# One copy of the split down weights and a third raw slot for down weights in a mixture-of-experts kernel

## The chip, the cores and the metric

The kernel runs on one core of a Trainium2 chip. The metric is the device time of one execution in microseconds; three runs of the kernel before are given, and the median counts. A core has TensorE (PE in the profile; its weight loads are PEld), VectorE (DVE), ScalarE (ACT) and GpSimd (POOL), each with a queue of its own that is worked in order. The sync engine (SP) computes nothing; it waits on semaphores and issues DMAs.

## What is computed

One layer of a streaming encoder over 1088 tokens of width 1024: an input LayerNorm, a token mixer (a state-space group and a short-convolution group), a projection with LayerNorm and router, a mixture of 64 experts with 6 per token, a shared expert, and a last LayerNorm. The change is about the routed experts:

```python
def expert_block(args):
    tok, e = args                       # the rows of 128 slots, one expert
    xb = h_pad[tok]
    hid = jax.nn.silu(xb @ w_gate[e]) * (xb @ w_up[e])
    return hid @ w_down[e]

yb = lax.map(expert_block, (row_tok.reshape(n_blocks, MOE_BLOCK), block_e))
yb = yb.reshape(rows, d) * row_w[:, None].astype(yb.dtype)
return jax.ops.segment_sum(yb, row_tok, num_segments=t + 1)[:t]
```

`w_gate[e]` and `w_up[e]` are 1024x256, `w_down[e]` is 256x1024, all float32: 1 MB each, 3 MB an expert. An expert gets one block of 128 slots or more, as its tokens need.

## The kernel before

The program is a row of stages with a barrier between them: trunk, mixing, output (gating and projection), experts, final LayerNorm. `expert_stage` (L1851) holds the loop.

A float32 product is made of three products in a reduced float format: a matrix is split into a high part (ScalarE copies it to the reduced type) and a low part (VectorE subtracts the high part from the original), and TensorE sums high x high, high x low and low x high. So every weight passes this way: DMA into a raw slot, high copy by ScalarE, low copy by VectorE, then matmuls from the two copies. A raw slot is free once the low part of its last block has been made.

- Raw slots: `raw_up` has `UP_SLOTS` = 3 slots (gate and up weights of one expert, 2 MB), `raw_dn` has `DN_SLOTS` = 2 (1 MB each). They are placed before `project_stage`, because that stage already fetches for the experts: `prefetch` (L1278) loads gate and up of experts 0 to 2 and down of experts 0 and 1.
- Split copies: `up_h`, `up_l` for two blocks (`par` is the block's parity), and `dn_h`, `dn_l` for two blocks as well.
- Experts are put in an order by `order_experts`; what is called expert e below is the one at place e. A table in `keep.small` tells each engine what block n needs: `THIRD` (its up slot, e mod 3), `ODD` (its down slot, e mod 2), the arrival counts `IN0` and `IN1`, `ENDS` (how many blocks there are up to the end of an expert) and `ORDER` (which expert stands at a place). `block_counts` (L1757) works the columns out on VectorE in a chain of small instructions, and TensorE turns them into rows (`turn_tables`).

Here the routing gives 77 blocks for 64 experts. `over_blocks` (L1898) runs `body(n)` for each block on every engine, each in its own order:

- TensorE: gate/up product of block n (`up`, 24 matmuls), transpose of the hidden values of n-1, transpose of the gathered tokens of n+2 (`turn_x`), down product of n-2 (`down`, 12 matmuls).
- ScalarE: SiLU of n (L1981), high hidden part of n-1, high token part of n+2 (L1992), high gate weights of n+2 (L1963, waits for the DMA of both gate and up weights), high down weights of n-1 (`down_high`, L2009), output copy of n-2 (L1986), high up weights of n+2 (L1963).
- VectorE: hidden values of n, low hidden part of n-1, low token part of n+2, low gate weights of n+2 (L2146), low down weights of n-1 (`down_low`, L2167), low up weights of n+2 (L2146).
- GpSimd: gather of the token rows of block n+4 (L2045), scatter with addition of the results of n-2 (L2054). Both are DMAs of GpSimd's own queue.
- SP: one expert at a time, and in order. For place e it first issues `down(e - 3)`, then `gate_up(e)`:

```python
def down(e, odd, until):
    expert = entry(sp, ORDER, e, N_EXP - 1)
    wait(sp, dn_l_done, until)
```

`until` is `ends(e - AHEAD)` with `AHEAD = UP_SLOTS + DN_SLOTS` = 5 for the down load at place e (L1937), and `ends(e - UP_SLOTS)` on `up_l_done` for the gate/up load (L1927). Each load also waits until the load two experts before it has arrived, since the two arrival semaphores are shared by parity.

`down_high(n)` waits with `wait(act, down_done, n - 1)`: the down product of block n-2, the last reader of its copy of `dn_h` and `dn_l`, must be over. In `project_stage` the scale and shift rows of the LayerNorm, `lng` and `lnb`, are two tensors of 128x1024; once the LayerNorms are done, parts of `lng` serve as scratch for the tables.

Of the kernel before, what the change touches and what calls it, by code (L numbers as in the profile page):

```python
# [6 lines left out]
ALU = mybir.AluOpType  # L7
# [6 lines left out]
P = 128  # L14
D = 1024
# [25 lines left out]
DN_SLOTS = 2  # L41
# [30 lines left out]
def chain(eng, own):  # L72


    count = {}

    def link(ins, sem=own):
        count[sem] = count.get(sem, 0) + 1
        ins.then_inc(sem, 1)
        eng.wait_ge(sem, count[sem])  # L80
    return link

# [1110 lines left out]
def project_stage(nc, io, keep, w, rt):  # L1193


    with ExitStack() as ctx:
        m = Pools(nc, ctx, "proj")
        gT, ycT = keep.gT, keep.ycT
        lng, lnb = m.sb("lng", [P, D]), m.sb("lnb", [P, D])
# [34 lines left out]
        whole, third, odd, both, in0, in1 = (m.sb(n, [P, 1]) for n in ("whole", "third", "odd", "both", "in0", "in1"))  # L1234
        even_i, evens, trip = m.sb("even_i", [1, 64], I32), m.sb("evens", [1, 64]), m.sb("trip", [1, 1])
# [30 lines left out]
        def _(sp):  # L1266
# [11 lines left out]
            def prefetch(e):  # L1278
# [5 lines left out]
                if e < DN_SLOTS:  # L1284
                    sp.dma_start(rt.raw_dn[:, e, :, :], io.w_down[0, e].rearrange("(p k) n -> p k n", p=P)).then_inc(
                        rt.down_in[e % 2], 16)
# [162 lines left out]
        def _(pe):  # L1449
# [98 lines left out]
            def turn_tables():  # L1548
                pe.wait_ge(s_eo, 1)
                for k, col in enumerate((in0, in1, third, odd)):  # L1550
# [44 lines left out]
        def _(v):  # L1595
# [161 lines left out]
            def block_counts():  # L1757

                for slot, n in ((third, UP_SLOTS), (odd, 2)):
# [3 lines left out]
                    link(stt(out=slot[:, :], in0=whole[:, :], scalar=-float(n), in1=eo[:, :], op0=ALU.mult, op1=ALU.add))  # L1763
                link(ts(both[:, :], eo[:, :], 8.0, 16.0, ALU.mult, ALU.add))
# [86 lines left out]
def expert_stage(nc, io, keep, rt):  # L1851

    with ExitStack() as ctx:
# [8 lines left out]
        dn_h, dn_l = m.sb("dn_h", [P, 2, 2, D], F32R), m.sb("dn_l", [P, 2, 2, D], F32R)  # L1862
# [20 lines left out]
        IN0, IN1, THIRD, ODD, ENDS, ORDER = range(6)  # L1883
# [39 lines left out]
        def _(sp):  # L1923
# [10 lines left out]
            def down(e, odd, until):  # L1934
# [5 lines left out]
                sp.dma_start(raw_dn[:, odd, :, :], w_d[bass.ds(expert, 1)].rearrange("a p k n -> (a p) k n")).then_inc(down_in[odd], 16)  # L1940
# [5 lines left out]
            LOOP = UP_SLOTS * DN_SLOTS  # L1946
            peeled = N_EXP - (N_EXP - AHEAD) // LOOP * LOOP
            for e in range(UP_SLOTS, peeled):
                if e >= AHEAD:
                    down(e - UP_SLOTS, (e - UP_SLOTS) % 2, ends(e - AHEAD))  # L1950
                gate_up(e, e % UP_SLOTS, e % 2, ends(e - UP_SLOTS))
            with sp.Fori(peeled, N_EXP - LOOP + 1, LOOP) as b:
                for u in range(LOOP):
                    e = peeled + u
                    down(b + (u - UP_SLOTS), (e - UP_SLOTS) % 2, ends(b + (u - AHEAD)))
                    gate_up(b + u, e % UP_SLOTS, e % 2, ends(b + (u - UP_SLOTS)))
            for e in range(N_EXP - UP_SLOTS, N_EXP):
                down(e, e % 2, ends(e - DN_SLOTS))

        @block.scalar  # L1960
        def _(act):
# [39 lines left out]
            def down_high(n, par):  # L2001
                in0, in1 = arrivals(act, n)
                slot = entry(act, ODD, n, DN_SLOTS - 1)
                wait(act, down_done, n - 1)
# [366 lines left out]
```

## Time and profile before

| | |
|---|---|
| device time, three runs | 1499.12, 1499.76, 1502.8 us; median 1499.76 |
| the profiled execution: span from first to last instruction | 1505.0 us; no other time of it is recorded |
| busy in the span: PE, DVE, ACT, POOL | 1278.8 us (85%), 1124.8 (75%), 875.4 (58%), 777.0 (52%) |
| expert loop, first to last SiLU | 662.87 to 1428.78 us |
| moved by DMA in the whole span | 334.94 MB |
| DMA issue to landing, median: gate, up, down weights | 9.3, 13.1, 8.1 us |
| the same for gathers, scatters | 11.4, 12.4 us |

Starts are us from the start of the span. A row of the timeline gives start, duration, engine, line and operation, and in brackets how long the engine was idle before it and what ended that. The busy share of the DMA is the mean over the core's 16 DMA engines of the time that packets were in flight there; with many transfers at once it reads a little over 1. TensorE's granted clock (PEclk) is a share of full speed.

### The profile page before, as it was taken

How to read it: one execution, taken by the hardware profiler on the slowest of the kernel's cores; microseconds unless marked ns; L12 is line 12 of the kernel's file. 1: busy time of each engine (PE TensorE's matmuls, PEld its weight loads, DVE VectorE, ACT ScalarE, POOL GpSimd, SP SyncE). 2: the span in 40 equal slices, each digit the busy share in tenths (PEclk: the TensorE clock that was granted, in tenths of full speed). 3: DMA queues.
4: the chain of work that ended last, by engine and by line, in shares of the span. 5: the costliest groups of instructions: out<-in, count | busy, mean ns of one | idle time of the engine just before them, and what ended most of it. 6: DMA issues, size and time to landing. Idle time of an engine off the chain costs nothing. (4 is left out here: it accounts for less than half of the span.)

```text
span 1505.0 us, 24140 instructions
## 1 busy us (share of the span) xinstructions
PE 1278.8 (85%) x6387; PEld 1086.6 (72%) x6387; DVE 1124.8 (75%) x1442; ACT 875.4 (58%) x1043; POOL 777.0 (52%) x643
## 2 busy tenths in 40 slices
PE   4787889986699989669999999999999999999920
PEld 3787888983488868558887778787877778787810
DVE  6925758743678976459988888887988888888828
ACT  7521201205535542148887778887877778887735
POOL 1017765804600136225765667676766667665720
PEclk9898989997799999879999999999999999999975
DMA  9233315256422354147899999999999989999647
GB/s 279 103 95 52 83 21 100 60 40 238 159 99 112 109 197 144 60 159 241 325 350 331 340 312 346 332 318 335 326 346 321 340 308 344 335 317 344 161 141 280
DMA packets 114164, 334.94 MB, mean 223 GB/s; under 512 B 30736, under 2 KB 61456, under 8 KB 89536
## 3 DMA queue, kind: packets, MB, share of 16 engines
q1 hardware_dynamic: 88928, 280.51, 52.5%
q0 software_dynamic: 24752, 53.73, 14.3%
q8 instruction: 26, 0.43, 0.1%
q14 instruction: 26, 0.21, 0.0%
q10 hardware_dynamic: 432, 0.07, 0.0%
HBM read 289.29 MB, written 71.14 MB: 239 GB/s over the span
## 5 line engine op out<-in xcount | busy, mean ns | idle before, releaser
L2146 DVE TENSOR_TENSOR moe_up_l<-rt_raw_up,moe_up_h 128x2048 fp32r<-128x2048 f32 x154 | 352.5, 2291 | 111.5 <-ACT moe_up_h L1963 111.4
L1963 ACT ACTIVATE moe_up_h<-rt_raw_up 128x2048 fp32r x154 | 294.1, 1912 | 123.0 <-DMA rt_raw_up<-in_w_up_dram 87.3
L2054 POOL DMA_INDIRECT acc<-moe_y,moe_idx_s x77 | 242.0, 3143 | 65.5 <-POOL moe_idx_s L2051 46.0
L2085 PE MATMUL moe_p_gu<-moe_up_h,moe_x_h 128*128 128x512 f32 x616 | 245.2, 398 | 2.6 <-DVE moe_x_l L2155 2.0
L2085 PE MATMUL moe_p_gu<-moe_up_l,moe_x_h 128*128 128x512 f32 x616 | 244.5, 397 | 0.0
L2085 PE MATMUL moe_p_gu<-moe_up_h,moe_x_l 128*128 128x512 f32 x616 | 244.4, 397 | 0.0
L2045 POOL DMA_INDIRECT moe_xg<-tok,moe_idx_g x79 | 161.6, 2046 | 63.6 <-POOL moe_idx_g L2042 61.8
L2167 DVE TENSOR_TENSOR moe_dn_l<-rt_raw_dn,moe_dn_h 128x2048 fp32r<-128x2048 f32 x77 | 176.0, 2285 | 4.8 <-ACT moe_dn_h L2009 4.7
L2051 POOL COPY moe_idx_s<-keep_small 128x1 int32 (+1 forms) x77 | 103.3, 1342 | 127.8 <-ACT moe_y L1986 127.8
L2097 PE MATMUL moe_p_dn<-moe_dn_h,moe_hid_h 128*128 128x512 f32 x308 | 132.1, 429 | 37.8 <-DVE moe_dn_l L2167 36.5
L2009 ACT ACTIVATE moe_dn_h<-rt_raw_dn 128x2048 fp32r x77 | 147.8, 1920 | 18.6 <-issue 8.1
L2085 PEld LDWEIGHTS moe_p_gu<-moe_up_h,moe_x_h 128*128 128x128 f32 x616 | 117.0, 190 | 32.0 <-DVE moe_x_l L2155 2.4
L2085 PEld LDWEIGHTS moe_p_gu<-moe_up_h,moe_x_l 128*128 128x128 f32 x616 | 116.3, 189 | 28.7
L2085 PEld LDWEIGHTS moe_p_gu<-moe_up_l,moe_x_h 128*128 128x128 f32 x616 | 116.6, 189 | 28.1
L1435 POOL DMA_INDIRECT slots<-proj_pay,proj_dst x54 | 55.4, 1026 | 156.8 <-DVE proj_dst L1682 142.8
L2097 PE MATMUL moe_p_dn<-moe_dn_l,moe_hid_h 128*128 128x512 f32 x308 | 125.1, 406 | 0.0
L2097 PE MATMUL moe_p_dn<-moe_dn_h,moe_hid_l 128*128 128x512 f32 x308 | 124.8, 405 | 0.0
L2155 DVE TENSOR_TENSOR moe_x_l<-moe_p_tr,moe_x_h 128x512 fp32r<-128x512 f32 x154 | 98.4, 680 | 7.3 <-ACT moe_x_h L1992 7.0
L775 PE MATMUL mix_proj<-co_hT_h,co_win_h 128*128 128x384 f32 (+1 forms) x288 | 97.9, 340 | 4.6 <-PEq L112 4.6
L2097 PEld LDWEIGHTS moe_p_dn<-moe_dn_h,moe_hid_h 128*128 128x128 f32 x308 | 60.6, 197 | 52.3 <-DVE moe_dn_l L2167 22.9
L775 PE MATMUL mix_proj<-co_hT_h,co_win_l 128*128 128x384 f32 (+1 forms) x288 | 96.6, 336 | 0.3 <-issue 0.3
L775 PE MATMUL mix_proj<-co_hT_l,co_win_h 128*128 128x384 f32 (+1 forms) x288 | 96.6, 335 | 0.0
(425 smaller groups left out, 2710.2 us busy)
## 6 DMA issues: line engine op xcount, KB each, us to landing
rt_raw_up<-in_w_gate_dram SPq DMA_DIRECT2D x64, 1024.0 KB, 9.3
rt_raw_up<-in_w_up_dram SPq DMA_DIRECT2D x64, 1024.0 KB, 13.1
rt_raw_dn<-in_w_down_dram SPq DMA_DIRECT2D x64, 1024.0 KB, 8.1
acc<-proj_ax SPq DMA_DIRECT2D x18, 512.0 KB, 2.6
final_x<-acc SPq DMA_DIRECT2D x18, 512.0 KB, 11.7
co_win<-in_w_in_dram SPq DMA_DIRECT2D x16, 512.0 KB, 4.9
resid<-trunk_x SPq DMA_DIRECT2D x9, 512.0 KB
proj_res<-resid SPq DMA_DIRECT2D x9, 512.0 KB
```

The source lines that it names most:

```text
L775: mm = pe.matmul(proj[:, pn % 3, 0:ln], a, b, start=(j == 0), stop=(j == len(terms) - 1))
L1435: pool.indirect_dma_start(out=io.slots, in_=pay[:, i, k, :], in_offset=None, out_offset=bass.IndirectOffsetOnAxis(ap=dst[:, i, k:k + 1], a ...
L1963: act.activation(up_h[:, par, half, :, :], raw_up[:, bass.ds(slot, 1), half, :, :].rearrange("p a k n -> p (a k) n"), ACT.Copy).then_inc(u ...
L2009: act.activation(dn_h[:, par, :, :], raw_dn[:, bass.ds(slot, 1), :, :].rearrange("p a k n -> p (a k) n"), ACT.Copy).then_inc(dn_h_done, 1)
L2045: pool.indirect_dma_start(out=xg[:, par, :], out_offset=None, in_=io.tok, in_offset=bass.IndirectOffsetOnAxis(ap=idx_g[:, par:par + 1], ax ...
L2051: pool.tensor_copy(idx_s[:, par:par + 1], rt.idx[:, at(n)]).then_inc(index_s, 1)
L2054: pool.indirect_dma_start(out=io.acc[par], in_=y[:, par, :], in_offset=None, out_offset=bass.IndirectOffsetOnAxis(ap=idx_s[:, par:par + 1] ...
L2085: mm = pe.matmul(p_gu[:, par, :].rearrange("p (a n) -> p a n", a=2), x, w, start=(i == 0), stop=(i == len(terms) - 1))
L2097: mm = pe.matmul(p_dn[:, h, :], a, w, start=(i == 0), stop=(i == len(terms) - 1))
L2146: low = tt(up_l[:, par, half, :, :], raw_up[:, bass.ds(slot, 1), half, :, :].rearrange("p a k n -> p (a k) n"), up_h[:, par, half, :, :].b ...
L2155: low = tt(x_l[:, par, 4 * h:4 * h + 4, :], p_tr[:, h, :].rearrange("p (k t) -> p k t", k=4), x_h[:, par, 4 * h:4 * h + 4, :].bitcast(F32) ...
L2167: tt(dn_l[:, par, :, :], raw_dn[:, bass.ds(slot, 1), :, :].rearrange("p a k n -> p (a k) n"), dn_h[:, par, :, :].bitcast(F32), ALU.subtrac ...
```

## The change

`DN_SLOTS` goes from 2 to 3. `dn_h` and `dn_l` are held once and not per parity, which frees 16 KB of each partition, and the third slot takes 8. `lng` and `lnb` have no tensors of their own any more: during the projection stage they lie in raw slot 0. The slots are filled from the top (`down_slot`: expert 0 in slot 2, expert 1 in slot 1, expert 2 in slot 0), so that the prefetch for experts 0 and 1 does not touch slot 0; expert 2's down weights are loaded at the head of the expert stage. `AHEAD` becomes 6. The table's column of the down slot is worked out from `third` with one more VectorE instruction.

```diff
-DN_SLOTS = 2
+DN_SLOTS = 3
+def down_slot(e):
+    return DN_SLOTS - 1 - e % DN_SLOTS
...
-        lng, lnb = m.sb("lng", [P, D]), m.sb("lnb", [P, D])
+        lng, lnb = rt.raw_dn[:, 0, 0, :], rt.raw_dn[:, 0, 1, :]
...
-                if e < DN_SLOTS:
-                    sp.dma_start(rt.raw_dn[:, e, :, :], io.w_down[0, e].rearrange("(p k) n -> p k n", p=P)).then_inc(
+                if e < DN_SLOTS - 1:
+                    sp.dma_start(rt.raw_dn[:, down_slot(e), :, :], io.w_down[0, e].rearrange("(p k) n -> p k n", p=P)).then_inc(
...
+                link(ts(dslot[:, :], third[:, :], -1.0, float(DN_SLOTS - 1), ALU.mult, ALU.add))
...
-        dn_h, dn_l = m.sb("dn_h", [P, 2, 2, D], F32R), m.sb("dn_l", [P, 2, 2, D], F32R)
+        dn_h, dn_l = m.sb("dn_h", [P, 2, D], F32R), m.sb("dn_l", [P, 2, D], F32R)
...
             AHEAD = UP_SLOTS + DN_SLOTS
-            LOOP = UP_SLOTS * DN_SLOTS
+            LOOP = UP_SLOTS * 2
             peeled = N_EXP - (N_EXP - AHEAD) // LOOP * LOOP
+            down(DN_SLOTS - 1, down_slot(DN_SLOTS - 1), (DN_SLOTS - 1) % 2, 0)
             for e in range(UP_SLOTS, peeled):
                 if e >= AHEAD:
-                    down(e - UP_SLOTS, (e - UP_SLOTS) % 2, ends(e - AHEAD))
+                    down(e - UP_SLOTS, down_slot(e - UP_SLOTS), (e - UP_SLOTS) % 2, ends(e - AHEAD))
                 gate_up(e, e % UP_SLOTS, e % 2, ends(e - UP_SLOTS))
...
             def down_high(n, par):
                 in0, in1 = arrivals(act, n)
-                slot = entry(act, ODD, n, DN_SLOTS - 1)
-                wait(act, down_done, n - 1)
+                slot = entry(act, DOWN, n, DN_SLOTS - 1)
+                wait(act, down_done, n)
...
-                    terms = [(a[:, par, k, :], w[:, par, k, cols]) for k in range(2)
+                    terms = [(a[:, par, k, :], w[:, k, cols]) for k in range(2)
```

On SP at the start of the expert stage the order is, before (trunk_x4 is the semaphore of the low gate/up copies, trunk_x6 that of the low down copies; the names are those of their first owners):

```order
L1922 UNCONDITIONAL_BRANCH [waits barrier_Pool_Activation_PE_DVE_SP_release]
...
L1931 ISA [waits trunk_x4,rt_up_in1]
L1931 DMA rt_raw_up<-in_w_gate_dram 128x2048
L1931 DMA rt_raw_up<-in_w_up_dram 128x2048
...
L1931 ISA [waits trunk_x4,rt_up_in0]
...
L1940 ISA [waits trunk_x6,rt_down_in0]
L1940 DMA rt_raw_dn<-in_w_down_dram 128x2048
```

and now:

```order
L1929 UNCONDITIONAL_BRANCH [waits barrier_Pool_Activation_PE_DVE_SP_release]
L1922 TENSOR_LOAD keep_small
L1922 ISA x2
L1947 ISA [waits rt_down_in0]
L1947 DMA rt_raw_dn<-in_w_down_dram 128x2048
...
L1938 ISA [waits trunk_x4,rt_up_in1]
L1938 DMA rt_raw_up<-in_w_gate_dram 128x2048
L1938 DMA rt_raw_up<-in_w_up_dram 128x2048
```

The down load of expert 2 moved ahead of the first gate/up load and lost its wait for the low down copies; in the loop itself the instructions stand in the same order, and only the value that the down load waits for is another.

On ScalarE, at the first down split (block 0), before:

```order
L1915 TENSOR_LOAD keep_small
L1915 ISA x2
L2009 ISA [waits rt_down_in0,rt_down_in1]
L2009 ACTIVATE moe_dn_h<-rt_raw_dn 128x2048
L1986 ACTIVATE moe_y<-moe_p_dn 128x1024 [waits co_wl]
L1963 ISA
L1963 ACTIVATE moe_up_h<-rt_raw_up 128x2048
```

and now (co_wl is the semaphore of the down products):

```order
L1922 TENSOR_LOAD keep_small
L1922 ISA x2
L2017 ISA [waits co_wl,rt_down_in0,rt_down_in1]
L2017 ACTIVATE moe_dn_h<-rt_raw_dn 128x2048
L1994 ACTIVATE moe_y<-moe_p_dn 128x1024 [waits co_wl]
L1971 ISA
L1971 ACTIVATE moe_up_h<-rt_raw_up 128x2048
```

No instruction moved; the down split of block n-1 now waits for the down product of n-2, as the output copy behind it does.

## Rows read from the trace of the kernel before

**Rows 1.** Timeline of ScalarE, SiLUs of six blocks: start us, us, engine, line, operation [idle before]
```profile
662.87 0.39 ACT L1981 ACTIVATE moe_sg<-moe_p_gu 128x256 f32<-128x256 f32 x1
748.25 0.36 ACT L1981 ACTIVATE moe_sg<-moe_p_gu 128x256 f32<-128x256 f32 x1
1013.58 0.38 ACT L1981 ACTIVATE moe_sg<-moe_p_gu 128x256 f32<-128x256 f32 x1
1023.02 0.37 ACT L1981 ACTIVATE moe_sg<-moe_p_gu 128x256 f32<-128x256 f32 x1
1348.93 0.37 ACT L1981 ACTIVATE moe_sg<-moe_p_gu 128x256 f32<-128x256 f32 x1
1428.78 0.38 ACT L1981 ACTIVATE moe_sg<-moe_p_gu 128x256 f32<-128x256 f32 x1 [4.00 <-PE moe_p_gu L2085]
```

**Rows 2.** Waits, 755 to 1355 us: waiter, releaser: us, times, longest
```profile
ACT moe_up_h L1963 <- DMA rt_raw_up<-in_w_up_dram: 75.3, 36, 5.5
PE moe_p_dn L2097 <- DVE moe_dn_l L2167: 27.5, 16, 3.8
```

**Rows 3.** Timeline of ScalarE and TensorE after a late weight load
```profile
1030.22 1.92 ACT L1963 ACTIVATE moe_up_h<-rt_raw_up 128x2048 fp32r x1 [5.53 <-DMA rt_raw_up<-in_w_up_dram]
1036.90 0.79 PE L2097 MATMUL moe_p_dn<-moe_dn_h,moe_hid_h 128*128 128x512 f32 x1 [3.42 <-DVE moe_dn_l L2167]
```

**Rows 4.** Waits of the sync queue (SPq), 755 to 1355 us
```profile
SPq L1937 <- DVE moe_dn_l L2167: 363.7, 50, 14.6
SPq L1927 <- DVE moe_up_l L2146: 8.6, 17, 0.7
```

**Rows 5.** Timeline of all engines, unstalled stretch, 1004 to 1019 us
```profile
1004.38 2.29 DVE L2146 TENSOR_TENSOR moe_up_l<-rt_raw_up,moe_up_h 128x2048 fp32r<-128x2048 f32 x1 [0.37 <-ACT moe_up_h L1963]
1011.19 2.28 DVE L2167 TENSOR_TENSOR moe_dn_l<-rt_raw_dn,moe_dn_h 128x2048 fp32r<-128x2048 f32 x1
1015.93 0.34 SPq L1931 DMA_DIRECT2D rt_raw_up<-in_w_gate_dram  x1
1016.38 1.92 ACT L1963 ACTIVATE moe_up_h<-rt_raw_up 128x2048 fp32r x1 [1.15 <-issue]
1016.46 0.39 PE L2097 MATMUL moe_p_dn<-moe_dn_h,moe_hid_l 128*128 128x512 f32 x1
1018.49 1.92 ACT L2009 ACTIVATE moe_dn_h<-rt_raw_dn 128x2048 fp32r x1 [0.19 <-DMA rt_raw_dn<-in_w_down_dram]
```

**Rows 6.** Stretch: us, busy PE, PEld, DVE, ACT, POOL (x); PEclk, DMA share, GB/s
```profile
755.00:1355.00 600.00, 572.17 (x2713) 472.49 (x2712) 512.20 (x414) 476.95 (x473) 404.61 (x237) 0.98 0.95 331
```

**Rows 7.** Stretches without the engines: us, PEclk, DMA share, GB/s
```profile
1035.00:1040.00 5.00, 0.68 0.58 174
1040.00:1075.00 35.00, 1.00 1.01 359
1245.00:1285.00 40.00, 1.00 1.01 343
```

**Rows 8.** Timeline of ScalarE and TensorE right after the stall
```profile
1040.76 1.93 ACT L2009 ACTIVATE moe_dn_h<-rt_raw_dn 128x2048 fp32r x1 [0.23 <-issue]
1041.05 0.39 PE L2097 MATMUL moe_p_dn<-moe_dn_h,moe_hid_l 128*128 128x512 f32 x1
1047.08 0.38 ACT L1981 ACTIVATE moe_sg<-moe_p_gu 128x256 f32<-128x256 f32 x1 [1.69 <-PE moe_p_gu L2085]
```

**Rows 9.** Timeline of TensorE at the start of the expert stage
```profile
648.81 1.55 PE L2104 MATMUL moe_p_tr<-keep_ident,moe_xg 128*128 128x128 f32 x6 [13.37 <-DMA moe_xg<-tok,moe_idx_g]
```

**Rows 10.** Timeline of VectorE in `block_counts`
```profile
624.06 0.15 DVE L1764 TENSOR_SCALAR proj_both<-proj_eo 128x1 f32<-128x1 f32 x1
```

**Rows 11.** A gather, its transposes, and the landings of all 79 gathers (L2045)
```profile
1018.61 3.04 POOL L2045 DMA_INDIRECT moe_xg<-tok,moe_idx_g  x1 [0.79 <-POOL moe_idx_g L2042]
1032.32 1.16 PE L2104 MATMUL moe_p_tr<-keep_ident,moe_xg 128*128 128x128 f32 x8 [0.19 <-DMA moe_xg<-tok,moe_idx_g]
DMA to landing us min/median/max: 4.2/11.4/13.6
```

More of the change, by code:

```diff
@@ L1234, in project_stage @@
         whole, third, odd, both, in0, in1 = (m.sb(n, [P, 1]) for n in ("whole", "third", "odd", "both", "in0", "in1"))
+        dslot = m.sb("dslot", [P, 1])
         even_i, evens, trip = m.sb("even_i", [1, 64], I32), m.sb("evens", [1, 64]), m.sb("trip", [1, 1])
@@ L1549, in turn_tables @@
                 pe.wait_ge(s_eo, 1)
-                for k, col in enumerate((in0, in1, third, odd)):
+                for k, col in enumerate((in0, in1, third, dslot)):
                     tr = pe.transpose(pt[0:1, 0, k * P:(k + 1) * P], col[:, 0:1], keep.ident[:, :])
@@ L1882, in expert_stage @@
         HEAD = 5
-        IN0, IN1, THIRD, ODD, ENDS, ORDER = range(6)
+        IN0, IN1, THIRD, DOWN, ENDS, ORDER = range(6)
         def wait(eng, sem, value):
@@ L1932, in gate_up, with down @@
                                  src[bass.ds(expert, 1)].rearrange("a p k n -> (a p) k n")).then_inc(up_in[odd], 16)
-            def down(e, odd, until):
+            def down(e, slot, odd, until):
                 expert = entry(sp, ORDER, e, N_EXP - 1)
@@ L1939, in down @@
                 sp.sem_inc(sp_go, 1)
-                sp.dma_start(raw_dn[:, odd, :, :], w_d[bass.ds(expert, 1)].rearrange("a p k n -> (a p) k n")).then_inc(down_in[odd], 16)
+                sp.dma_start(raw_dn[:, slot, :, :], w_d[bass.ds(expert, 1)].rearrange("a p k n -> (a p) k n")).then_inc(down_in[odd], 16)
             def ends(e):
@@ L1954, in _ @@
                     e = peeled + u
-                    down(b + (u - UP_SLOTS), (e - UP_SLOTS) % 2, ends(b + (u - AHEAD)))
+                    down(b + (u - UP_SLOTS), down_slot(e - UP_SLOTS), (e - UP_SLOTS) % 2, ends(b + (u - AHEAD)))
                     gate_up(b + u, e % UP_SLOTS, e % 2, ends(b + (u - UP_SLOTS)))
             for e in range(N_EXP - UP_SLOTS, N_EXP):
-                down(e, e % 2, ends(e - DN_SLOTS))
+                down(e, down_slot(e), e % 2, ends(e - DN_SLOTS))
         @block.scalar
@@ L2008, in down_high @@
                 act.sem_inc(act_go, 1)
-                act.activation(dn_h[:, par, :, :], raw_dn[:, bass.ds(slot, 1), :, :].rearrange("p a k n -> p (a k) n"),
+                act.activation(dn_h[:, :, :], raw_dn[:, bass.ds(slot, 1), :, :].rearrange("p a k n -> p (a k) n"),
                                ACT.Copy).then_inc(dn_h_done, 1)
@@ L2164, in down_low @@
             def down_low(n, par):
-                slot = entry(v, ODD, n, DN_SLOTS - 1)
+                slot = entry(v, DOWN, n, DN_SLOTS - 1)
                 wait(v, dn_h_done, n + 1)
-                tt(dn_l[:, par, :, :], raw_dn[:, bass.ds(slot, 1), :, :].rearrange("p a k n -> p (a k) n"),
-                   dn_h[:, par, :, :].bitcast(F32), ALU.subtract).then_inc(dn_l_done, 1)
+                tt(dn_l[:, :, :], raw_dn[:, bass.ds(slot, 1), :, :].rearrange("p a k n -> p (a k) n"),
+                   dn_h[:, :, :].bitcast(F32), ALU.subtract).then_inc(dn_l_done, 1)
             def body(n, par, more):
```

## Prediction

> **What bounds the kernel now.** I read first how far apart the blocks of the expert loop are, then who waits there, then the sync queue, and last the rate of the transfers. One SiLU (L1981) marks each of the 77 blocks [rows 1]. From the first (662.87 us) to the last (1428.78) there are 76 steps and 765.9 us, 10.08 us a step. Where nothing stalls a step is 9.44 us (1013.58 to 1023.02), and there TensorE issues without a gap, so 9.44 is its own time for a block. 76 x 9.44 = 717.4, so the loop loses 48.5 us. The loss is not spread evenly: 748.25 to 1348.93 is 59 steps and 600.7 us, 43.7 over its 557.0; the nine steps before lose 0.4 and the eight after 4.3.
>
> Within 755 to 1355, TensorE waits 27.5 us for the low part of the down weights and ScalarE 75.3 us for the up weights' DMA [rows 2]. One case shows how they hang together [rows 3]: ScalarE splits the next up weights at 1030.22 after 5.53 us idle, of which 1.15 are its register loads [rows 3, 5], so the data is 4.4 us late; everything behind that on ScalarE and VectorE slides, the down split with it, and TensorE starts the down product at 1036.90 after 3.42 us idle, its matmul then 0.79 us long where 0.39 is usual [rows 3, 5]; the granted clock, 1.00 before, stands at 0.68 over these five us [rows 7], a mean with a part at the 1.2 GHz level, right after the idle. A late weight load is the root.
>
> Why is it late? The sync queue spends 363.7 of these 600 us at L1937, the down load's wait for a free raw slot, and 8.6 at L1927, the gate/up load's own wait [rows 4]. The queue is in order, so the gate/up load stands behind the down load. In numbers [rows 5]: the late weights are expert X's, loaded by the issue at 1015.93. Their slot had last been read by the up_l that started at 1004.38 and ended at 1006.67 (with 3 slots the expert 3 before X ends at block 35, and that instruction serves block 35). The load ahead of it waited for the dn_l of block 33, started at 1011.19, ended 1013.47; then 2.5 us of issue and register loads until 1015.93. At the unstalled pace ScalarE would want the weights one step after 1016.38, at 1025.8. So the load has 9.9 us where its slot allowed 19.2.
>
> What does a load need? The transfers moved 331 GB/s over the 600 us, 198.6 MB, at a busy share of 0.95 [rows 6]. Where the share was 1.01 the rate was 359 GB/s in one stretch and 343 in another [rows 7]. The down loads that waited there are 50 [rows 4], and 50 experts of 3.15 MB are 157.3 MB; the rest, 41.3 MB, is 0.70 MB of gather and scatter for each of the 59 blocks. A one-block expert is then 3.85 MB, 10.7 us at 359: more than 9.9, less than 19.2. A two-block expert is 4.55 MB, 12.7 us in 18.9 us of TensorE time; there the engines of the DMA run dry today.
>
> **The change, part by part.**
> (1) Third raw slot: L1937 waits for the expert 6 before and not 5. In a run of one-block experts that is one block, 9.44 us, earlier: for X it ends before its slot is free. The gate/up load then goes at its own slot's release, or some 2.5 us after the down load's if that is later, up to 9.3 us earlier, and the down loads 9.4 us earlier. 9.3 us of lead against a deficit of 10.7 - 9.44 = 1.3 us per one-block expert covers a run of seven. 77 blocks for 64 experts are 13 second blocks, one in about five experts, and each two-block expert gives back 18.9 - 12.7 = 6.2 us. So the loop becomes limited by averages, not by single loads. The floors for the 59 steps: TensorE 557.0 us; DMA 198.6 MB at 359 GB/s 553, at 343 GB/s 579. I take 351, the middle of the two, since both stretches are saturated and mix gathers and weights: 566 us. Two streams so near each other do not overlap perfectly, and I add 4 us (an allowance; a tenth of today's 43.7): 570. Gain 600.7 - 570 = 31 us; its bounds are 600.7 - 557 = 44 and, at 343 with the same allowance, 18. Of the tail's 4.3 us, which starts with the same late loads, I take 3.
>
> The Trainium skill (HBM Reference, Specifications) gives about 358 GB/s per core when both cores of a domain stream; 198.6 MB at that is 555 us as an estimate, near the 553 above. The Trainium skill (DMA: Bandwidth & Descriptors, Bandwidth) lists 341 GB/s for a single 1 MB transfer, the size of all these loads; that would be 582 us, against the change. The 359 GB/s row stands above it, so here 1 MB loads that queue behind each other run faster than that.
>
> (2) One copy of dn_h/dn_l. ScalarE's down split now waits for the down product one block later. Unstalled, the last down matmul starts at 1016.46 and ends 1016.85; the split starts at 1018.49 [rows 5], so the wait is over 1.6 us before it is asked, and ScalarE cannot come sooner, since x_high and an up split, both behind the same transposes, stand ahead. After a stall, with TensorE in part at the low clock, the product ends at 1041.44 and the split began at 1040.76 [rows 8]: 0.7 us later with the change. Behind it are y_out, an up split and the next SiLU; that SiLU found 1.69 us idle, which takes it. If that cover were gone it would be 0.7 us in each of the stalled blocks, about 16: 11 us. VectorE's and TensorE's waits keep their counts. Cost 0; bounds 0 to 11.
>
> (3) Down weights of expert 2 are loaded as the first act of the expert stage. They are 1.05 MB, 2.9 us at 359, beside the first gathers, for which TensorE waits until 648.81 [rows 9]. Bounds 0 (the gather is on another queue) to 2.9 (it stands behind the whole load); I take 1, nearer to the first, since both queues are served at once elsewhere in the loop.
>
> (4) The slot table: one VectorE instruction of 128x1 in the chain, 0.15 us [rows 10]. Upper bound 0.2, taken. Scale rows in a raw slot: same instructions, same sizes, 0.
>
> Sum: 31 + 3 - 0 - 1 - 0.2 = 33 us (32.8). Against the profiled span: 1505.0 - 33 = 1472. The runs' median lies 5.2 us under that span, outside the terms here, so the forecast is 1499.8 - 33 = 1467.
>
> **Rivals.**
> A, the DMA ceiling is low: once loads queue, the rate stays at 343 or under, as in one saturated stretch. The middle then takes 579 to 583 and the gain is 18, 1482. For it: the share is already 0.95. Against: 359 at the same share in the other row [rows 7].
> B, slower, by the gathers. A gather is issued at 1018.61 and its transposes come at 1032.32, with 0.19 us of waiting for it [rows 11]: 13.5 us of lead, and the landings go up to 13.6. The lead is two steps less what lies between, so each us of landing above 13.5 stretches a step by 0.5. With weights always queued, gathers share the DMA engines with them all the time. At a landing of 15.0 us each step gains 0.75, which is 44 us in 59 steps: the whole gain. From there on it is slower; at 15.3, 9 us more, 1509. Against: the landings of 11.4 in the middle already come from saturated stretches mostly. The Trainium skill (DMA: Bandwidth & Descriptors, Queues, rings and completion order) says each DMA engine takes turns between queues packet by packet; by that, a longer weight queue does not delay a gather more than a short one, which the row's narrow top (11.4 to 13.6) agrees with.
> C, it doesn't bring loads forward: the wait moves from L1937 to L1927, the gate/up load's own slot, and the lead stays. For it: L1927 is already waited for. Against: the slot stood free from 1006.67 to 1015.93 [rows 5]. It gives 1498, between 1495 and 1500.
> D, the DMA reaches 359 throughout: the loop runs at TensorE's pace, 44 + 4 - 1 = 47 us off, 1453.
>
> **How the numbers follow.** Forecast 0.6 (1467, itself 1460 to 1477), A 0.19, D 0.09, C 0.08, B 0.04. The range 1452 to 1486 takes in D, the forecast and A and leaves out B, C and what of A lies above. Faster by over 0.3% (4.5 us, about what a measurement of this kernel can tell from none): forecast, A, D and a part of C, 0.90; within 0.3%: 0.06; slower: 0.04.
>
> **What would show it.** L1937's wait falls from 364 us to below 100 and that of L1927 grows to well over 100. In the middle the DMA's rate rises from 331 to about 348 GB/s, share near 1.0. ScalarE's wait for the up weights falls from 75 to under 25 and TensorE's for dn_l from 27.5 to under 8. The low clock vanishes from most of the loop, steps of 13.8 us are gone, and SiLU to SiLU is 735 us in all. The down split (L2009 before) shows no long waits for TensorE. It is wrong if these waits fall and others take their place: gathers with TensorE behind them (B), or the same rate at a share of 1.0 (A).

## The result and the profile after

The changed kernel takes 1488.95 us (median of four runs, 1487.22 to 1489.92) against 1501.28 us for the kernel before, run beside it (four runs, 1499.12 to 1505.73). The ratio is 0.9919, with a 95% interval of 0.9895 to 0.9942: faster by 12 us, where 33 were forecast. 1488.95 lies above the forecast range (1452 to 1486). The profiled executions are 1505.0 and 1487.4 us long, 17.6 us apart. A span is about 1.7 us shorter than the device time of the same run (1487.4 for 1489.15), so the profiled run of before was some 5 us slower than the median of its kind, and that of the changed kernel was at its median. The parts below therefore add up to 17.6 and not to 12.3, and each difference from the profile of before carries some of these 5 us.

Line numbers are 7 or 8 higher after the change. The SiLUs of blocks 0, 9, 68 and 76, on ScalarE's timeline (columns as in [rows 1]):

```profile
661.88 0.39 ACT L1989 ACTIVATE moe_sg<-moe_p_gu 128x256 f32<-128x256 f32 x1
...
747.29 0.37 ACT L1989 ACTIVATE moe_sg<-moe_p_gu 128x256 f32<-128x256 f32 x1
...
1329.16 0.37 ACT L1989 ACTIVATE moe_sg<-moe_p_gu 128x256 f32<-128x256 f32 x1
...
1405.77 0.39 ACT L1989 ACTIVATE moe_sg<-moe_p_gu 128x256 f32<-128x256 f32 x1 [2.51 <-PE moe_p_gu L2093]
```

The 59 middle steps take 581.9 us, where [rows 1] gave 600.7; they still lose 24.9 over TensorE's 557.0. The last eight take 76.6 instead of 79.9, the first nine 85.4 as before. The waits of the compute engines and of the sync queue, 755 to 1355 us, and the stretches:

```profile
ACT moe_up_h L1971 <- DMA rt_raw_up<-in_w_up_dram: 69.1, 44, 3.8
PE moe_p_dn L2105 <- DVE moe_dn_l L2175: 16.4, 13, 2.3
...
ACT moe_dn_h L2017 <- PE moe_p_dn L2105: 1.5, 1, 1.5
```

```profile
SPq L1934 <- DVE moe_up_l L2154: 198.0, 52, 11.3
SPq L1944 <- DVE moe_dn_l L2175: 148.4, 34, 4.7
SPq L1936 <- DMA rt_raw_up<-in_w_up_dram: 20.5, 15, 2.5
```

```profile
747.29:1329.16 581.87, 566.62 (x2716) 469.44 (x2716) 512.95 (x413) 478.91 (x473) 411.48 (x236) 0.99 0.96 341
970.00:980.00 10.00, 10.00 (x50) 8.30 (x49) 7.50 (x8) 7.50 (x9) 7.21 (x5) 1.00 0.67 218
1240.00:1250.00 10.00, 10.00 (x50) 8.28 (x50) 9.26 (x8) 8.66 (x10) 6.76 (x4) 1.00 0.57 186
```

What is to be seen: the down load's wait for a slot (L1937 before, L1944 now) fell from 364 to 148 us, and that of the gate/up load (L1934) took its place. ScalarE still waits 69 us for up weights, more often (44 times, not 36) and for shorter times, the longest 3.8 us and not 5.5. About 1.15 us of each such wait are register loads, so the sum overstates how late the weights are: the up splits that waited longer than that (19 of them before and 19 now, 755 to 1355 us) waited 36 us beyond it before and 24 us now. The DMA carried 341 GB/s over the 59 steps, where it was 331 [rows 6]. In two stretches of 10 us at experts with two blocks it has too little to do (share 0.67 and 0.57). The page's list of issues shows the other side, with the median us to landing in the last column; for up and down it was 13.1 and 8.1 before:

```profile
rt_raw_up<-in_w_gate_dram SPq DMA_DIRECT2D x64, 1024.0 KB, 9.3
rt_raw_up<-in_w_up_dram SPq DMA_DIRECT2D x64, 1024.0 KB, 19.2
rt_raw_dn<-in_w_down_dram SPq DMA_DIRECT2D x64, 1024.0 KB, 17.1
```

Expert X of the prediction (place 32) shows what that means. Before, its load was issued at 1015.93 and ScalarE began at 1030.22. Now the timelines of SyncE and ScalarE give, for places 32 and 33 and the high splits that use them:

```profile
996.36 0.33 SPq L1938 DMA_DIRECT2D rt_raw_up<-in_w_gate_dram  x1
...
1005.81 0.33 SPq L1938 DMA_DIRECT2D rt_raw_up<-in_w_gate_dram  x1
```

```profile
1015.13 1.92 ACT L1971 ACTIVATE moe_up_h<-rt_raw_up 128x2048 fp32r x1 [1.14 <-DMA rt_raw_up<-in_w_up_dram]
...
1025.83 1.92 ACT L1971 ACTIVATE moe_up_h<-rt_raw_up 128x2048 fp32r x1 [2.38 <-DMA rt_raw_up<-in_w_up_dram]
```

X now has 18.8 us of lead (19.2 were forecast) and is in time. The next expert has as much lead, but its split begins only 20.0 us after the issue, 1.2 us late. The lead nearly doubled (9.9 to 18.8 us), and the landing grew with it (median 13.1 to 19.2 us for the up load).

The second difference is the end. From the last SiLU to the first load of the final stage it was 1428.78 to 1453.95, 25.2 us; now it is 1405.77 to 1437.46, 31.7. Down splits, down products and output copies of the last two blocks, timeline of all engines after the change:

```profile
1409.04 1.91 ACT L2017 ACTIVATE moe_dn_h<-rt_raw_dn 128x2048 fp32r x1 [2.61 <-PE moe_p_dn L2105]
...
1413.44 0.80 PE L2105 MATMUL moe_p_dn<-moe_dn_h,moe_hid_h 128*128 128x512 f32 x1 [4.47 <-DVE moe_dn_l L2175]
...
1418.91 1.91 ACT L2017 ACTIVATE moe_dn_h<-rt_raw_dn 128x2048 fp32r x1 [6.77 <-PE moe_p_dn L2105]
...
1423.31 0.79 PE L2105 MATMUL moe_p_dn<-moe_dn_h,moe_hid_h 128*128 128x512 f32 x1 [4.70 <-DVE moe_dn_l L2175]
...
1428.78 1.02 ACT L1994 ACTIVATE moe_y<-moe_p_dn 128x1024 f32<-128x1024 f32 x1 [7.04 <-PE moe_p_dn L2105]
```

The last split waits 6.8 us for the down product before it, then VectorE's low copy follows, then TensorE's product. Nothing is left to lie beside this chain, and the matmuls at its start take 0.80 us. In the kernel before, the last split had no wait; it began even before the product of the block ahead of it, which ran from 1436.21 to 1440.8:

```profile
1434.80 1.91 ACT L2009 ACTIVATE moe_dn_h<-rt_raw_dn 128x2048 fp32r x1
...
1436.21 0.80 PE L2097 MATMUL moe_p_dn<-moe_dn_h,moe_hid_h 128*128 128x512 f32 x1 [4.24 <-DVE moe_dn_l L2167]
```

The sum of the 17.6 us: first SiLU 1.0 earlier, middle 18.8, last eight steps 3.2, final stage 1.1 shorter, end 6.5 longer.

### The profile page after: what moved, and what is told of

It is laid out like the page before. It is cut to its first block and busy times, and to the rows that moved or that the text cites. A ratio compares the mean times of both kernels' runs of the same rounds, so it can differ in the third digit from the quotient of the medians.

```text
span 1487.4 us, 24146 instructions
## 1 busy us (share of the span) xinstructions
PE 1274.6 (86%) x6387; PEld 1083.6 (73%) x6387; DVE 1126.9 (76%) x1443; ACT 876.7 (59%) x1043; POOL 783.4 (53%) x643
## 5 line engine op out<-in xcount | busy, mean ns | idle before, releaser
L2053 POOL DMA_INDIRECT moe_xg<-tok,moe_idx_g x79 | 165.1, 2090 | 63.6 <-POOL moe_idx_g L2050 61.8
L2059 POOL COPY moe_idx_s<-keep_small 128x1 int32 (+1 forms) x77 | 107.2, 1393 | 106.9 <-ACT moe_y L1994 106.9
L2093 PEld LDWEIGHTS moe_p_gu<-moe_up_h,moe_x_h 128*128 128x128 f32 x616 | 116.5, 189 | 31.7 <-DVE moe_x_l L2163 2.4
L2112 PE MATMUL moe_p_tr<-keep_ident,moe_xg 128*128 128x128 f32 x616 | 82.8, 278 | 15.5 <-DMA moe_xg<-tok,moe_idx_g 13.4
## 6 DMA issues: line engine op xcount, KB each, us to landing
rt_raw_up<-in_w_up_dram SPq DMA_DIRECT2D x64, 1024.0 KB, 19.2
rt_raw_dn<-in_w_down_dram SPq DMA_DIRECT2D x64, 1024.0 KB, 17.1
final_x<-acc SPq DMA_DIRECT2D x18, 512.0 KB, 13.1
```

What stands on the lines that cost most here:

```text
L2053: pool.indirect_dma_start(out=xg[:, par, :], out_offset=None, in_=io.tok, in_offset=bass.IndirectOffsetOnAxis(ap=idx_g[:, par:par + 1], ax ...
L2059: pool.tensor_copy(idx_s[:, par:par + 1], rt.idx[:, at(n)]).then_inc(index_s, 1)
L2093: mm = pe.matmul(p_gu[:, par, :].rearrange("p (a n) -> p a n", a=2), x, w, start=(i == 0), stop=(i == len(terms) - 1))
L2112: tr = pe.transpose(p_tr[:, k // 4, (k % 4) * P:(k % 4 + 1) * P], xg[:, par, k:D:KD], keep.ident[:, :])
```

## Experiments

All times are medians, each beside runs of the kernel before on the same chip (medians of 1500.2 to 1503.9 us in four groups of runs); a ratio is against those. Stretches, waits and ends come from one profiled run of each kernel. "Middle" is SiLU 9 to SiLU 68, "loop" SiLU 0 to 76, "end" the last SiLU to the final stage's first load.

**1. What the single copy costs alone.** The kernel before, with two raw slots, and only this:

```diff
-        dn_h, dn_l = m.sb("dn_h", [P, 2, 2, D], F32R), m.sb("dn_l", [P, 2, 2, D], F32R)
+        dn_h, dn_l = m.sb("dn_h", [P, 2, D], F32R), m.sb("dn_l", [P, 2, D], F32R)
...
-                wait(act, down_done, n - 1)
+                wait(act, down_done, n)
```

> The kernel before with one part of the change alone: dn_h and dn_l held once, the down split waiting one down product later, still two raw slots and the old order of loads. Theory (a serial end): in the loop the wait costs nothing, but behind the last block nothing else runs, so down product, down split high, split low and the last down product follow each other, and from the last SiLU to the first load of the final stage it takes 31 to 32 us and not 25. Total 1505 to 1508 us where before is 1500, the loop from first to last SiLU unchanged at 764 to 768. Rival (the wait is free everywhere, the longer end of the changed kernel has another cause, the transfers): 1499 to 1502, the end 25 us. Rival (the wait costs in the loop after each stall): over 1510, the loop above 770.

It took 1506.83 us against 1501.04, ratio 1.0042 (1.0019 to 1.0064). In its profile the loop is 758.9 us, no longer than that of before (it is even shorter than the 764 to 768 expected; this profiled run was 3.5 us faster than its median, that of before some 5 us slower), and the end 30.6 (1419.97 to 1450.60) where it was 25.2. No cost of the single copy shows in the loop, and it costs 5 to 6 us behind it. The changed kernel is this kernel plus the third slot and what goes with it: 1488.95 against 1506.83, so by the medians the third slot gives some 18 us, and the single copy takes back some 6.

**2. The end mended.** The changed kernel, with the down split of the last block but one put into a half of `up_h` and `up_l` that no later block needs:

```diff
+        def down_copy(own, up, where):
+            if where != "second":
+                return own[:, :, :]
+            return up[:, 1, 0, :, :].rearrange("p k n -> p (k n)").rearrange("p (a n) -> p a n", a=2)
...
-                wait(act, down_done, n)
+                if where != "second":
+                    wait(act, down_done, n - 1 if where == "last" else n)
```

> The changed kernel, but the down weights of the last block but one are split into the half of up_h and up_l that is free by then, so that the last two down splits no longer wait for each other's down product. Theory (serial end): the end falls from 31.7 us to about 26, total 1483 to 1484 (changed kernel 1489, before 1501). Rival (the end is long for another reason): same as the changed kernel within 1.5 us.

1483.69 us (1482.01 to 1484.4), ratio 0.9887 (0.9868 to 0.9907): 5.3 us under the changed kernel, as the theory said, and the lowest median of the kernels that do all the work (experiment 8, at 1485.37, cannot be told from it). The end is 24.2 us (1406.95 to 1431.12). On ScalarE's timeline neither of the last two splits waits for a product any more:

```profile
1409.28 1.91 ACT L2024 ACTIVATE moe_up_h<-rt_raw_dn 128x2048 fp32r x1 [1.66 <-issue]
...
1412.83 1.91 ACT L2024 ACTIVATE moe_dn_h<-rt_raw_dn 128x2048 fp32r x1 [0.46 <-issue]
```

**3. Order instead of a slot.** The kernel before with two slots, and gate/up issued ahead of the down load at each place:

```diff
-                    down(b + (u - UP_SLOTS), (e - UP_SLOTS) % 2, ends(b + (u - AHEAD)))
                     gate_up(b + u, e % UP_SLOTS, e % 2, ends(b + (u - UP_SLOTS)))
+                    down(b + (u - UP_SLOTS), (e - UP_SLOTS) % 2, ends(b + (u - AHEAD)))
```

> The kernel before, two raw slots and two split copies, with only the order on the sync queue turned: gate and up load of expert e first, then the down load of e-3. Theory (only the place in the queue mattered): the gate/up load goes at its own slot's release as in the changed kernel, the end stays at 25 us, so the time is that of the changed kernel or better: 1480 to 1489. Rival (the third slot's room is what helped, it lets more be under way): 1494 or more, since nothing holds more than before.

1493.62 us, ratio 0.9958 (0.9944 to 0.9972). The middle is 587.0 us, at 339 GB/s. One exchanged pair of lines, with no memory spent, gives 7.4 us, where the changed kernel gives 12.3 and that of experiment 2 gives 17.4. That lies between the two sides: less than the theory had expected and hardly more than the rival's bound. The late loads are now the down weights (755 to 1355 us); the longest wait for up weights is 1.2 us, the register loads alone:

```profile
ACT moe_dn_h L2009 <- DMA rt_raw_dn<-in_w_down_dram: 41.4, 18, 3.5
...
ACT moe_up_h L1963 <- DMA rt_raw_up<-in_w_up_dram: 20.7, 18, 1.2
```

**4. Both together, with the end mended.** The edits of 2 and 3 on the changed kernel.

> The changed kernel with the short end and the gate/up load ahead of the down load, three down slots. Theory (order: the down load, issued a block before it is needed, stands 3 us ahead of gate and up weights that are needed first): ScalarE's wait for the up weights falls, the loop by 5 to 9 us, total 1475 to 1479 against 1484 of the kernel with the short end alone. Rival (slots): whatever comes first, the same bytes are short in the same blocks; what is saved at the up weights comes back at the down weights, total 1482 to 1485.

1490.27 us, ratio 0.9935 (0.9912 to 0.9957), 6.6 us above experiment 2 and above what either side had expected. The middle is 588.8 us at 338 GB/s. The two do not add up. Behind the gate/up load the down load waits for nothing of its own (755 to 1340 us: SyncE waits 358.9 us on the low gate/up copies, none on the low down copies), it now stands behind the load that is blocked, and it comes late (ScalarE waits 47.0 us for it).

**5. Separate arrival counts.** The changed kernel, with gate and up weights counted by semaphores of their own, so that the gate split need not wait for the up load:

```diff
-            rt.up_in = [r.sem("up_in0"), r.sem("up_in1")]
+            rt.up_in = [[r.sem("gate_in0"), r.sem("gate_in1")], [r.sem("up_in0"), r.sem("up_in1")]]
```

> The changed kernel with arrival counts of their own for gate and for up weights: the split of the gate weights waits for the gate load alone, that of the up weights, 4.8 us later in ScalarE's row, for the up load. Theory (joint wait: the remaining stalls come from waiting for the up load too early): ScalarE's wait for the up load in the middle (69 us in 44 waits) falls under 20, the 59 steps of the middle from 582 to 563-570 us, total 1470 to 1477. Rival (slots: in the two-block experts all three up slots are full and the DMA stands idle 5 to 7 us, and the loads of the run that follows are late by the same total): the lateness moves but the total falls by 3 to 6 us only, 1483 to 1486. Rival (the transfer rate is the limit): no gain, 1488 to 1490.

1489.08 us, ratio 0.9928 (0.9906 to 0.9951): no change against the changed kernel, as the last rival said. ScalarE's wait for up weights turned into a wait for gate weights (54.0 us, 35 times, 755 to 1340 us), whose landing is now given as 17.5 us and not 9.3. The 9.3 was read from a count that both loads raise, so it said little of the gate load itself: the gate weights come nearly as late as the up weights (in experiment 8, with separate counts too, 20.7 and 20.9 us), and the joint wait cost nothing that the total shows. The rate is 341 GB/s as before.

**6. Four gate/up slots.** One copy of the down splits, two down slots, four gate/up slots, gate/up first, and the down weights of experts 0 and 1 loaded at the head of the expert stage; then the same with the end mended:

```diff
-UP_SLOTS = 3
+UP_SLOTS = 4
...
+            gate_up(UP_SLOTS - 1, UP_SLOTS - 1, (UP_SLOTS - 1) % 2, 0)
+            down(0, 0, 0)
+            down(1, 1, 0)
```

> Where the room is spent: one copy of dn_h and dn_l and two raw slots for down weights as before, but four raw slots for gate and up weights instead of three, the gate/up load ahead of the down load on the sync queue; in the projection stage its scratch lies in the down slots, so that the down weights of experts 0 and 1 are loaded at the head of the expert stage. Uses as much memory as the kernel before. Theory (slots: in two-block experts the three gate/up slots are full and the DMA stands idle, and the run after is late by the same total): the DMA's idle stretches at the two-block experts shrink, the busy share of the middle rises from 0.96 to 1.00 and over, first to last SiLU falls from 744 us to 722-730, total 1470 to 1477 (it still has the long end). Rival (the transfer rate is the limit at 343 GB/s): loop 740 to 745, total 1487 to 1491.

> The same with the last down split but one in the free half of up_h and up_l, as in the run with the short end. Theory (slots): 5 us below the run without it, 1465 to 1472. Rival (rate is the limit): 1482 to 1486, the time of the changed kernel with the short end.

1500.93 us, ratio 0.9995 (0.9974 to 1.0016), and 1494.88 with the end mended, 0.9964 (0.9945 to 0.9983). Both lie above what either side had expected. The second repeats the 6 us of the end. In the first, the middle is 587.2 us at 337 GB/s, the same as with the exchanged order alone (experiment 3), so the fourth slot added nothing there; the waits are for down weights (43.0 us). It also pays at the start, which neither side had counted: the first SiLU is 5 us later and the nine steps behind it take 88.4 us and not 85.4. That slots for gate/up were what is missing fell, at least in this form and this order of loads.

**7. Without the down loads.** The changed kernel with no down load from expert 3 on.

> The changed kernel without the loads of down weights from expert 3 on (the arrival count is raised by the sync engine, the slots keep the weights of experts 0 to 2, so the results differ from the reference): 61 MB less to move. Theory (all that the loop still loses is weights that come late): every step is 9.44 us, first to last SiLU 717 to 720 us against 744, total 1462 to 1466. Rival (the loop loses to something else, gathers or the engines' own chain): the loop stays above 730 us.

1465.37 us against 1500.22, ratio 0.9768 (0.9737 to 0.98). The kernel leaves out 61 loads of 1 MB. The loop takes 718.7 us and the middle 558.2, every step of it 9.4 to 9.5. The stretch view, and ScalarE's wait for up weights (755 to 1340 us):

```profile
755.00:1340.00 585.00, 585.00 (x2845) 487.22 (x2844) 538.40 (x435) 501.11 (x497) 482.54 (x248) 1.00 0.81 263
```

```profile
ACT moe_up_h L1974 <- DMA rt_raw_up<-in_w_up_dram: 45.9, 40, 1.2
```

So all that the changed kernel's middle still loses goes with the 61 loads that are missing here: it is weights that come late. The single copy and the engines' own chain cost nothing there. TensorE waits for no gather here, and for 0.3 us in the changed kernel; that gathers and scatters take their part of the DMA's time, and so delay weights, is not excluded, since here they had more room. The row of ScalarE is 45.9 us although nothing is late: it is 40 times the register loads. The end is 32.2 us here too.

**8. Half a slot given back at a time.** Experiment 2 with separate counts, and the gate half of a slot free as soon as its own low copy is made; in the second kernel the down load stands between gate and up load, which is the order in which VectorE gives the buffers back:

```diff
-                wait(sp, up_l_done, until)
-                sp.sem_inc(sp_go, 1)
-                for half in range(2):
...
+                for half, src in enumerate((w_g, w_u)):
+                    if half and between:
+                        between()
+                    wait(sp, (gate_l_done, up_l_done)[half], until)
...
-                if 1 in halves:
-                    low.then_inc(up_l_done, 1)
+                    low.then_inc((gate_l_done, up_l_done)[half], 1)
```

> The changed kernel, all of its work, with three edits: the tail edit (last two down splits in two buffers), separate arrival counts for gate and up, and each half of a raw gate and up slot given back when its own low half is made, so that the gate load of a later expert may be issued some 4.9 us ahead of the up load (order in the queue as in the changed kernel: down weights, gate, up). Room theory (the loop still loses time because no slot is free at the experts with two blocks, where the DMA share falls to 0.6): the gate loads come earlier, the share over the 59 middle steps rises from 0.96 to 0.97 or more, the middle falls from 582 to 570-576, the loop from 744 to 730-738, total 1474-1480. Rate theory (343 to 350 GB/s over the stretch is what 16 DMA engines give with this mix, whatever room there is): middle 579-583, total 1482-1486, the wait only moves from one load to another.

> As the kernel before it in this call, with one more edit: the queue's order of an expert is gate, down weights of three experts earlier, up, which is the order in which VectorE gives the three buffers back in a step with one block. Room theory: the down load no longer holds back a gate load whose half is free, middle 566-574, total 1470-1479, and less wait of SyncE on the down split than 148 us in 34. Rate theory: no change against the kernel before it within 3 us. Order theory (down loads must stand ahead, as the two turned kernels showed): ScalarE waits more for down weights (over 15 us in the middle) and the loop is 3 to 6 us longer than with down weights ahead.

1485.37 us, ratio 0.9879 (0.9859 to 0.9898), and 1486.26, 0.9876 (0.9856 to 0.9896). The first filled the gaps it was made for, but not with the gain that the room theory gave. In the second ScalarE waits 42.4 us for down weights, as the order theory said, but the loop is only 2.0 us longer and the total 0.9, within the 3 us of the rate theory. One stretch at a two-block expert, first the changed kernel, then experiment 8:

```profile
965.00:985.00 20.00, 20.00 (x92) 16.52 (x92) 17.16 (x15) 15.99 (x16) 13.25 (x9) 0.94 0.83 263
```

```profile
965.00:985.00 20.00, 20.00 (x99) 16.61 (x98) 18.25 (x17) 16.30 (x17) 13.51 (x11) 1.00 0.97 322
```

And the whole middle of it:

```profile
746.33:1332.07 585.74, 569.23 (x2716) 471.28 (x2716) 513.88 (x413) 481.24 (x473) 416.90 (x236) 0.99 0.98 339
```

The gap at the two-block expert is filled, the share rose from 0.96 to 0.98, and the rate is 339 GB/s, no more than before (341). Cut into 116 slices of 5 us (755 to 1335), the changed kernel has 12 slices with a share under 0.8 and this one 2, while the mean of the slices with a share of 0.99 or more fell from 366 (76 slices) to 355 GB/s (69). What was gained in the gaps was lost in the full slices. Why these got slower is not settled.

**9. More bytes and fewer.** Experiment 8 with one load of 256 KB more for each expert, into a buffer that nobody reads, and then with a quarter of each down matrix left out:

```diff
+                sp.dma_start(spare[:, odd, :], w_d[bass.ds(expert, 1)].rearrange("a p k n -> (a p) k n")[:, 0, 0:512]).then_inc(extra_in[odd], 16)
```

```diff
+                n = D if isinstance(e, int) and e < DN_SLOTS else 768
+                sp.dma_start(raw_dn[:, slot, :, 0:n],
+                             w_d[bass.ds(expert, 1)].rearrange("a p k n -> (a p) k n")[:, :, 0:n]).then_inc(down_in[odd], 16)
```

> The changed kernel with the tail edit, separate arrival counts and half a slot given back at a time (as e12_half), and one load more for each expert from 3 on: 256 KB of down weights into a buffer that nobody reads, issued between the down load and the gate load with no wait for a slot. It adds 0.26 MB to some 46 experts between SiLU 9 and 68, 12 MB beside 199. Rate theory (about 340 GB/s is all that the DMA engines give with this mix): the middle goes from 585.7 to 616-624 us (12 MB at 340 GB/s is 35), the mean rate stays at 335-345, total 1519-1527. Slots theory (the engines could carry 355 to 367 if only more were queued, what is missing are free slots): the middle goes up by 0 to 15 us, the mean rate to 350 or more, total 1485-1502.

> As e12_half, but from expert 3 on three quarters of each down matrix are loaded (columns 0 to 767), so the last quarter of the down product's columns uses weights of an earlier expert. That is 12 MB less in the middle, in the same number of loads. Rate theory: the middle falls by as much as 12 MB take at 340 GB/s, 35 us, but not below TensorE's 557-558: 558-564, total 1457-1466. Slots theory: each expert still waits for the same slots, which come free at VectorE's pace, the middle falls by 10-20 us only: 566-576, total 1466-1476.

1520.01 us (ratio 1.0123, 1.0091 to 1.0155) and 1459.43 us (0.9721, 0.969 to 0.9751). Their middles, more and less:

```profile
747.16:1360.71 613.55, 577.21 (x2712) 475.98 (x2712) 512.85 (x413) 480.13 (x473) 401.89 (x236) 0.97 0.98 344
```

```profile
749.73:1307.89 558.16, 558.16 (x2717) 464.90 (x2716) 513.60 (x413) 482.85 (x473) 460.56 (x236) 1.00 0.97 332
```

With more bytes (344 x 613.55 = 211.1 MB, 12.5 more) the middle is 27.8 us longer: 2.5 us short of the rate theory's band, 13 above the slots theory's. Bytes are what costs, but not at a fixed 340 GB/s: the 12.5 MB went through at 450, and the mean rose to 344. With fewer (332 x 558.16 = 185.3 MB; a quarter of the down product then uses the wrong weights) it stops at 558.2, TensorE's own time, as the rate theory said, and needs 332 GB/s for that. The full 198.6 MB in 557 us would be 357 GB/s. No kernel of this study had more than 344 over its middle; at 344 the full bytes would take 577 us, so of the 24.9 us that the changed kernel still loses some 20 are the rate and 5 the arrangement, by this estimate.

## Why the prediction was wrong

Two terms of the sum failed: the DMA floor of the middle (gain 31, measured 18.8 in the profiles) and the cost 0 of the single copy (6.5 in the profiles). The other terms are small.

**Direction and mechanism: right.** The late gate/up loads were the root, the down load's wait blocked them in the queue, and the third slot took most of that away (363.7 to 148.4 us): experiment 3 reaches part of it by order alone, experiment 7 shows that nothing but late weights holds the middle. The lead of X was forecast as 19.2 and is 18.8.

**The DMA floor: the term that was mis-sized.** I took 351 GB/s, midway between a saturated stretch at 359 and one at 343 [rows 7], for a floor of 566 us, and 4 us for imperfect overlap: 570, a gain of 31. The middle is 581.9 at 341 GB/s, a gain of 18.8. The rate at full share was read as what the DMA keeps up as a mean. It does keep it up while the share is full: the 5-us slices at a share of 0.99 or more average 358 GB/s before (71 of the 116 slices from 755 to 1335 us) and 366 after (76). But the mean of the middle holds gaps too, and where experiment 8 filled them the full slices fell to 355. The kernels with all their loads, whether with three down slots, four gate/up slots or another order, have a middle of 582 to 591 us at 335 to 341 GB/s, with shares from 0.94 to 0.98. What holds the mean there is open; no run varied the gathers and scatters or the size of a load. The arithmetic "9.3 us of lead covers seven experts" used the same 359 and failed with it: a one-block expert's 3.85 MB take 11.3 us at 341, a deficit of 1.85 and not 1.3 us, so the lead covers five, and the landing rose to 20 us. For the middle this is rival A's number ("the rate stays at 343 or under", middle 579 to 583, gain 18), which I gave 0.19, though not quite its mechanism, since the slices at full share run above 343. The Trainium skill (DMA: Bandwidth & Descriptors, Bandwidth) has 341 GB/s for one transfer of 1 MB, measured with transfers that GpSimd issues, and I set it aside since 359 stood above it. The loads here are SyncE's. The measured mean is 341 as well; that the reason is the size of a load is shown by no run here.

**The single copy: cost 0 in the loop, right; 6.5 us behind it, missed.** Rows 5 and 8 were read for the steady loop only, and there the split waits for a product once (1.5 us). The step "ScalarE cannot come sooner, since x_high and an up split stand ahead" is true of a body with a block n+2. The last two bodies have none, and the loop's drain has no SiLU, gather or up split beside which the wait could lie. Experiments 1 (+5.8), 2 (-5.3) and 6 (-6.1) price it three times. With A's 18 in the place of 31, and 6.5 for the end, my sum gives 13.3, and the medians moved by 12.3. That they agree so well is partly luck: the profiles, from which both numbers are taken, moved by 17.6.

**The small terms.** Last eight steps: 3 forecast, 3.2. Start: 1 us lost was forecast and 1.0 gained; single starts of these kernels lie between 660.1 and 664.9 us with the same head of the stage (experiments 2, 7, 8 and 9), so neither sign is shown. The final stage's 1.1 is of that size too.

**The signs.** L1937's wait under 100: 148. L1927's over 100: 198, right. Rate 348: 341, and share near 1.0: 0.96. ScalarE's wait under 25: 69, but this sign was badly chosen, since the same row is 45.9 in experiment 7, where no weight is late. TensorE's under 8: 16.4. The granted clock of the middle rose from 0.98 to 0.99. Steps of 13.8 gone: yes, the longest is 12.2. SiLU to SiLU 735: 743.9. Rival B (gathers) fell: their landings are 4.0, 11.4 and 13.3 us, as [rows 11] had them, and TensorE waits 0.3 us for them in all (755 to 1355 us). Rival C fell with the changed lead, and D was reached by no kernel that loaded all weights.

## What to carry to other kernels

When loads come late, first work out which mean rate the loop would need in order to be bound by compute, and set it beside the mean rate, not the best stretch, of a part where the DMA is already busy. Here 357 were needed and before there were 331 at a share of 0.95; every arrangement of slots then ended at 335 to 341 and 582 to 591 us. Before memory is spent on another slot, try the order of the queue; one exchanged pair gave 7.4 us here where the change gave 12.3, though the two did not add up. And when a double buffer is made single, read the last two rounds of the loop by themselves: the wait that the steady loop hid here was paid where it drains, and a buffer that was dead by then could stand in. And a sum of waits is a sign only once it is known what it is when nothing is late.

## What was not expected of the hardware

The busy share was no measure of what is left. From 0.96 to 0.98 it rose with no change of the rate, and without the down loads it was 0.81 at 263 GB/s: a rate lower by 23% with 16% less share (341 and 0.96 in the changed kernel).

The two kinds of transfer did not use the DMA's time alike. In the changed kernel's middle the views give, as packets, MB and share of the 16 engines' time, for the sync queue's weights (q1) and GpSimd's gathers and scatters (q0):

```profile
q1 hardware_dynamic: 21548, 156.94, 68.0%
q0 software_dynamic: 16982, 41.73, 28.1%
```

Over 581.87 us that is 397 GB/s of busy time for weights and 255 for gathers and scatters (384 and 257 before, 383 and 255 in experiment 8). Of the two stretches of [rows 7] the one at 359 GB/s carried 2.32 of its 12.56 MB as gathers and scatters, 18%, the one at 343 carried 2.93 of 13.72, 21%, as the middle does. So part of the distance between the two rows may be their mix; no run varied it.

Lead given to a load was eaten by its landing here. For the up load, which closes the shared count, the landing went from 13.1 to 19.2 us with the change, and for the down load from 8.1 to 17.1; with the slots given back by halves (experiment 8) it was 20.9 and 21.1, with 256 KB more for each expert (experiment 9) 22.9 and 23.0, with 256 KB less 14.0 and 12.9, always for loads of 1 MB, or three quarters of it for the last number.

TensorE paid for the drained end twice. In the changed kernel its first matmuls after waits of 4.47 and 4.70 us take 0.80 and 0.79 us, and most of both products runs at 0.63 us a matmul where 0.39 is usual; the granted clock over that stretch is 0.66, a mean with parts at the 1.2 GHz level. The mended kernel (experiment 2) pays it once, as the kernel before did (0.80 us after 4.24 us idle), at the product before the last (0.79 us after 3.53 us idle); before the last product it waits 1.29 us and the first matmul takes 0.47, and the clock over the stretch is 0.89. The stretch view of the changed and of the mended kernel, and the latter's last product on TensorE's timeline:

```profile
1409.00:1429.00 20.00, 10.52 (x24) 7.59 (x24) 4.92 (x3) 6.14 (x6) 5.94 (x4) 0.66 0.23 33
```

```profile
1409.00:1425.00 16.00, 8.48 (x30) 6.10 (x29) 4.92 (x3) 7.06 (x6) 5.34 (x6) 0.89 0.31 44
```

```profile
1419.31 0.47 PE L2113 MATMUL moe_p_dn<-moe_dn_h,moe_hid_h 128*128 128x512 f32 x1 [1.29 <-ACT moe_y L2000]
```
